# Merged gate halves: turned by TensorE, or moved in 32 wide blocks by three DMA queues and turned by VectorE

## The chip, the core and the metric

The kernel runs on one core of one Trainium2 chip. TensorE, VectorE (DVE), ScalarE (ACT), GpSimd (POOL) and SyncE (SP) each run their own list of instructions in order and meet at semaphores. The metric is the device time of one execution in microseconds (us); lower is better.

## What is computed

Two layers of a decoder trunk, 256 tokens of width 1024, all in float32. The change lies in the middle of each layer, where two branches are gated, added and projected:

```python
z = h @ w_in[l]
y_a = gmlp_branch(...) @ gm_w_proj[l]
y_b = mla_branch(...) @ mla_w_proj[l]
gates = jax.nn.sigmoid(z[..., OFF_GATE:].reshape(B, S, N_BRANCHES, D))
merged = gates[..., 0, :] * y_a + gates[..., 1, :] * y_b
x = x + merged @ w_out[l]
h2 = rms_norm(x, ffn_norm_g[l])
if l % 2 == 0:
    x = x + swiglu(h2, ...)            # dense, layer 0
else:
    x = x + moe_swiglu(h2, ...)        # top 2 of 8 experts, layer 1
```

## The kernel before

**Products.** Each float32 matrix is held as a high part (rounded to the matmul's type) and a low part (the rest), and a product is three passes: high x high, low x high, high x low. Weights come in chunks of 128 x 2048 numbers. SyncE loads a chunk into a ring of raw slots, ScalarE copies it to `w_hi` (`split_hi`, line 549), VectorE subtracts to get `w_lo` (`split_lo`, line 554), and TensorE multiplies (`one_pass`, line 619). In the mixer a chunk holds four 128-row tiles for a strip of 512 columns, so it is 2 (token tiles) x 4 x 3 = 24 matmuls. `w_hi` and `w_lo` have three slots: the copy of chunk n + 3 waits until TensorE is done with chunk n (`chunk_used`). A raw slot is loaded again when the subtraction of its last chunk is done (`lo_done`).

**Order.** `plan` is one hand-written list of steps. TensorE, ScalarE and VectorE each walk it in order and do their share of every step. `mul(l, what, j, k0, then, inside)` adds a chunk to the plan: the matmuls, then the steps of `then`, then `("split", ...)` for the chunk three further on. GpSimd and SyncE have programs of their own.

**The stretch in question.** Tokens lie on the partitions, 128 x 2 tiles. The last projection `pb` gives two strips (halves) of 512 columns. `evac("pb", j)` on VectorE (lines 2004 to 2013) scales strip j by its gate and adds it to `vbuf`, and raises `merged_b`. The product with `w_out` needs the operand with its 1024 columns on the partitions, so each half must be turned. `("merged_turns", l, half)` does that: TensorE turns eight 128 x 128 tiles into two PSUM banks (line 1018, through `turn4`, line 932), ScalarE copies them with the factor 0.5 to `act_hi` (line 1419), VectorE subtracts to `act_lo` (line 1866). Half 0 is turned after chunk `pb(1, 0)`, half 1 after chunk `wo(0, 0)`. The four chunks of `w_out` are multiplied in the order (strip 0, rows 0 to 511), (strip 1, rows 0 to 511), (strip 0, rows 512 to 1023), (strip 1, rows 512 to 1023); the first two read half 0 of the operand, the last two half 1.

**Who else hangs on it.** In layer 0, GpSimd waits for `merged_b`, clears `ws_raw` and stores it 18 times to `x_rows` and `y_rows` in HBM (lines 868 to 880), before it moves the hidden blocks of the dense layer for VectorE to turn (line 888). In layer 1 it waits for `merged_b` and loads the router's weights `wr`, `br` (lines 892 to 896), for which the step `("router", l)` of ScalarE and VectorE waits. SyncE's first expert load into memory that the mixer used waits until half 1 of layer 1 has been turned (lines 531, 532).

Of the kernel before, what the change touches and what calls it, by code (L numbers as in the profile page):

```python
# [34 lines left out]
P = 128  # L35
# [23 lines left out]
def decoder_trunk(nc, x, mix_norm_g, w_in, gm_v_norm_g, gm_v_norm_b, gm_w_spatial, gm_b_spatial, gm_w_proj,  # L59
# [72 lines left out]
    keys_in = {}  # L132

    def mul(l, what, j, k0=0, then=(), split=True, inside=()):
# [15 lines left out]
        else:  # L150
# [19 lines left out]
    for l in range(L):  # L170
# [113 lines left out]
    with ExitStack() as ctx:  # L284
# [53 lines left out]
        def part(n):  # L338
# [43 lines left out]
        vv = sb("vv", [P, TT, H, DV], F32, mixer)  # L382
        ws_t = sb("ws_t", [P, NG, P], F32, mixer)
# [92 lines left out]
            sem("scores_done"), sem("max_ready"), sem("exp_done"), sem("prob_ready"))  # L476
        merged_b, sig_done = sem("merged_b"), sem("sig_done")
# [10 lines left out]
        chosen_ready, gap_ready, places_read, counts_ready = (  # L488
            sem("chosen_ready"), sem("gap_ready"), sem("places_read"), sem("counts_ready"))
# [7 lines left out]
        class Ring:  # L497
# [23 lines left out]
            def wait_slot(self, sp, e, j):  # L521
# [105 lines left out]

        def turns_in(step):
            return {"norm_turns": 2, "latent_turns": 2 - step[2] if step[0] == "latent_turns" else 0, "spatial_weights": 2, "mix_tokens": 2, "merged_turns": 2,
# [36 lines left out]
        def operand_turns(l, what, k0):  # L666
# [8 lines left out]
                    "wo": lambda: last_turn["merged_turns", l, half]}.get(what, lambda: None)()  # L675
# [50 lines left out]
        def _(sp):  # L726
# [19 lines left out]

            for n in range(2):
# [1523 lines left out]
```

## Time and profile before

| | |
|---|---|
| median of 3 runs | 1414.89 us (1413.83 to 1415.05) |
| the profiled execution | 1415.23 us |
| its span, first to last instruction | 1413.5 us |
| TensorE matmul / weight load busy | 99% / 82% |
| VectorE, ScalarE, GpSimd busy | 83%, 67%, 12% |
| granted TensorE clock, mean | 0.999 |
| bytes moved | 424.32 MB, 300 GB/s |

How to read it: the expert phase takes about the last 750 us of the span, the two mixers and the dense layer the rest. In the views PE is TensorE's matmuls, PEld its weight loads, SPq the queue of SyncE. A row of a timeline is start, duration, engine, line, operation, output<-inputs, count, and in brackets the idle time before it and what ended it. Where neighbours are merged, the duration is that of the group.

### The profile page before, as it was taken

The page shows a single profiled execution, that of the slowest core. Times are in us where ns is not written, and L with a number is a line of the kernel's source. Part 1 is how long each engine was busy: PE and PEld are TensorE (multiplying, and loading weights), DVE is VectorE, ACT ScalarE, POOL GpSimd, SP SyncE. Part 2 cuts the span into 40 slices and gives each one's busy share as a digit, 9 for nine tenths or more (in the row PEclk, how much of TensorE's full clock was granted, in tenths as well). Part 3 has the DMA queues.
Part 4 walks back from the last instruction along what each step waited for, and adds up shares of the span by engine and source line. Part 5 has one row for each costly group of instructions (what it writes and reads, how often), then busy time and mean ns, then how long its engine had stood idle before and what let it go on. Part 6 is the DMA issues. An engine that isn't in the chain of part 4 may idle for free.

```text
span 1413.5 us, 19089 instructions
## 1 busy us (share of the span) xinstructions
PE 1404.5 (99%) x6567; PEld 1159.6 (82%) x6567; DVE 1167.7 (83%) x1197; ACT 950.0 (67%) x966; POOL 172.1 (12%) x305
## 2 busy tenths in 40 slices
PE   9999999999999999999999999999999999999998
PEld 7888778888888888788888888888888888888886
DVE  6998766676557899667989898898988988999986
ACT  6678645445435677644777777777777777778774
POOL 2032003476600050000300000000000000000010
PEclk9999999999999999999999999999999999999999
DMA  9476549976666484558999999999999999999995
GB/s 338 163 217 207 179 150 332 300 228 201 200 222 206 155 245 128 194 179 314 330 355 410 365 396 408 373 390 405 351 410 372 385 405 365 393 371 393 409 374 188
DMA packets 171636, 424.32 MB, mean 300 GB/s; under 512 B 19436, under 2 KB 50792, under 8 KB 171544
## 3 DMA queue, kind: packets, MB, share of 16 engines
q1 hardware_dynamic: 157128, 393.42, 76.7%
q0 software_dynamic: 13376, 26.16, 6.1%
q10 hardware_dynamic: 1040, 3.68, 0.6%
q8 instruction: 38, 0.62, 0.2%
q14 instruction: 54, 0.44, 0.1%
HBM read 398.20 MB, written 15.81 MB: 293 GB/s over the span
## 4 chain that ended last, share of the span: by engine, by line
PE 96%; DMA 2%; DVE 1%; ACT 0%; SPq 0%; issue 0%; DVEq 0%; ACTq 0%
PE ps L619 89%; DMA raw_more<-in_moe_w_down 1%; PE ps L1194 1%; PE ps L1053 1%; PE ps L1062 1%; PE ps L932 1%; PE ps L1051 1%; PE ps L1037 1%; PE ps L1010 0%; PE ps L976 0%; DMA raw<-in_w_in 0%; DVE w_lo L554 0%; ACT w_hi L549 0%; PE ps L1035 0%; PE ps L1186 0%; SPq L537 0%
## 5 line engine op out<-in xcount | busy, mean ns | idle before, releaser
L554 DVE TENSOR_TENSOR w_lo<-raw,w_hi 128x2048 fp32r<-128x2048 f32 (+3 forms) x184 | 383.7, 2092 | 78.0 <-ACT w_hi L549 76.9
L549 ACT ACTIVATE w_hi<-raw 128x2048 fp32r<-128x2048 f32 (+3 forms) x184 | 322.2, 1758 | 123.7 <-PE ps L619 97.5
L619 PE MATMUL ps<-w_hi,act_hi 128*128 128x512 f32 (+1 forms) x1264 | 332.4, 391 | 0.6 <-DVE w_hi L1803 0.5
L619 PE MATMUL ps<-w_hi,act_lo 128*128 128x512 f32 (+1 forms) x1264 | 328.5, 387 | 0.0
L619 PE MATMUL ps<-w_lo,act_hi 128*128 128x512 f32 (+1 forms) x1264 | 326.8, 387 | 0.0
L619 PEld LDWEIGHTS ps<-w_lo,act_hi 128*128 128x128 f32 x1264 | 235.8, 188 | 48.2
L619 PEld LDWEIGHTS ps<-w_hi,act_lo 128*128 128x128 f32 x1264 | 235.6, 188 | 48.0
L619 PEld LDWEIGHTS ps<-w_hi,act_hi 128*128 128x128 f32 x1264 | 233.1, 188 | 46.9 <-ACT act_hi L1337 1.2
L554 DVE TENSOR_TENSOR w_lo<-raw_more,w_hi 128x2048 fp32r<-128x2048 f32 (+1 forms) x96 | 201.8, 2110 | 30.4 <-ACT w_hi L549 30.4
L549 ACT ACTIVATE w_hi<-raw_more 128x2048 fp32r<-128x2048 f32 (+1 forms) x96 | 170.0, 1775 | 56.1 <-PE ps L619 46.8
L554 DVE TENSOR_TENSOR w_lo<-raw_low,w_hi 128x2048 fp32r<-128x2048 f32 (+1 forms) x64 | 137.6, 2156 | 13.4 <-ACT w_hi L549 12.7
L549 ACT ACTIVATE w_hi<-raw_low 128x2048 fp32r<-128x2048 f32 (+1 forms) x64 | 115.9, 1810 | 38.2 <-PE ps L619 33.4
L554 DVE TENSOR_TENSOR w_lo<-raw_lent,w_hi 128x2048 fp32r<-128x2048 f32 (+3 forms) x56 | 119.9, 2140 | 19.5 <-ACT w_hi L549 19.4
L549 ACT ACTIVATE w_hi<-raw_lent 128x2048 fp32r<-128x2048 f32 (+3 forms) x56 | 100.6, 1797 | 32.2 <-PE ps L619 31.6
L619 PE MATMUL ps<-w_hi,ehid_hi 128*128 128x512 f32 x352 | 96.6, 392 | 0.0
L619 PE MATMUL ps<-w_lo,ehid_hi 128*128 128x512 f32 x352 | 95.8, 390 | 0.4 <-DVE w_lo L554 0.4
L619 PE MATMUL ps<-w_hi,ehid_lo 128*128 128x512 f32 x352 | 95.8, 389 | 0.0
L888 POOL DMA_DIRECT2D hid_blocks<-hid x176 | 86.0, 497 | 62.5 <-DVE hid L2031 48.5
L913 POOL DMA_INDIRECT xres<-y_rows,row_i x4 | 8.2, 2050 | 670.4 <-PE ps L619 670.4
L619 PEld LDWEIGHTS ps<-w_lo,ehid_hi 128*128 128x128 f32 x352 | 65.9, 188 | 14.9 <-DVE w_lo L554 1.3
L619 PEld LDWEIGHTS ps<-w_hi,ehid_lo 128*128 128x128 f32 x352 | 66.1, 188 | 13.9
L619 PEld LDWEIGHTS ps<-w_hi,ehid_hi 128*128 128x128 f32 x352 | 65.4, 188 | 13.1
(296 smaller groups left out, 1353.3 us busy)
## 6 DMA issues: line engine op xcount, KB each, us to landing
raw<-in_moe_w_gu SPq DMA_DIRECT2D x96, 512.0 KB, 11.7
raw_more<-in_moe_w_down SPq DMA_DIRECT2D x80, 512.0 KB, 10.9
raw<-in_w_in SPq DMA_DIRECT2D x66, 512.0 KB, 5.4
raw_low<-in_moe_w_gu SPq DMA_DIRECT2D x64, 512.0 KB, 12.1
raw_more<-in_moe_w_gu SPq DMA_DIRECT2D x64, 512.0 KB, 12.3
raw<-in_moe_w_gu SPq DMA_DIRECT2D x48, 384.0 KB, 8.4
raw<-in_dense_w_gu SPq DMA_DIRECT2D x34, 512.0 KB, 5.3
raw_lent<-in_moe_w_gu SPq DMA_DIRECT2D x32, 512.0 KB, 11.3
```

The lines of the kernel that those rows point to most:

```text
L549: nc.scalar.activation(w_hi[:, self.split_slot(j), 0:n], self.raw(j)[:, 0:n], ACT.Copy).then_inc(self.hi, 1)
L554: nc.vector.tensor_tensor(w_lo[:, c, 0:n], self.raw(j)[:, 0:n], w_hi[:, c, 0:n].bitcast(F32), ALU.subtract).then_inc(self.lo, 1)
L619: return nc.tensor.matmul(dst, a, b, start=start and n == 0, stop=stop and n == 2)
L888: pool.dma_start(hid_blocks[32 * c:32 * c + 32, j % 2, b, :], hid_by_block[32 * b:32 * b + 32, j % 2, c, :, :, :]).then_inc(hid_moved[j % ...
L913: pool.indirect_dma_start(xres[:, t, :], None, y_row_list, bass.IndirectOffsetOnAxis(ap=row_i[:, 1, c, t:t + 1], axis=0), compute_op=ALU.a ...
L932: mm = nc.tensor.transpose(bank[:, i * P:(i + 1) * P], src(i // TT, i % TT), ident)
L1037: nc.tensor.matmul(dst.rearrange("p (t q) -> p t q", t=TT), vv[:, t, 2 * n + hh, :], first_keys[hh], start=True, stop=False)
L1051: nc.tensor.matmul(ps[:, 6, hh * P:(hh + 1) * P].rearrange("p (b i) -> p b i", b=4), q_h[:, 0:P], k_h[:, 0:4, :], start=True, stop=True)
L1053: mm = nc.tensor.matmul(ps[:, 7, hh * S:(hh + 1) * S].rearrange("p (b i) -> p b i", b=8), q_h[:, P:S], k_h, start=True, stop=True)
L1062: mm = nc.tensor.transpose(bank[:, q * P:(q + 1) * P], probs[pair % 2][:, blk * P:(blk + 1) * P], ident)
L1194: mm = nc.tensor.transpose(turn_banks(j)[:, k * P:(k + 1) * P], ehid[:, k * P:(k + 1) * P], ident)
```

## The change

The halves are no longer turned by TensorE. VectorE writes the sum of the gated strips not to `vbuf` but to `merged_by_block`, a view of `u_buf` in which the columns are ordered by blocks of 32. Sixteen DMAs a half, each 32 partitions x 1 KB, move the blocks to their place in `merged_turned`, a view of `qb`: three of them issued by GpSimd, six by SyncE, seven by ScalarE. VectorE then turns every 32 x 32 block with one transpose of 128 x 1024 in place (`merged_blocks`); ScalarE copies the result to `act_hi` and VectorE subtracts to `act_lo` (`merged_split`). The factor 0.5 is applied when the product with `w_out` is added to `x`. GpSimd's fill in layer 0 waits for the second transpose, SyncE's first expert load into mixer memory for `m_lo`. Two semaphores of the router are made one.

The diff, without declarations, the router's semaphores and the removed branches of `merged_turns`:

```diff
+        if (what, k0) == ("wo", 4):
+            moves_at[l, j] = len(chunks) - 1
...
         mul(l, "pb", 0, 4, [evac("pb", 0)])
-        mul(l, "pb", 1, 0, [("merged_turns", l, 0)])
-        mul(l, "pb", 1, 4, [evac("pb", 1)])
-        mul(l, "wo", 0, 0, [("merged_turns", l, 1)] + [("router", l)] * (l % 2))
-        mul(l, "wo", 1)
+        plan.append(("merged_moves", l, 0))
+        mul(l, "pb", 1, 0, [("merged_blocks", l, 0)])
+        mul(l, "pb", 1, 4, [("merged_split", l, 0), evac("pb", 1)])
+        plan.append(("merged_moves", l, 1))
+        mul(l, "wo", 0, 0, [("router", l)] * (l % 2))
+        mul(l, "wo", 1, 0, [("merged_blocks", l, 1), ("merged_split", l, 1)])
...
-                    wait_turn_read(sp, last_turn["merged_turns", L - 1, 1])
-                    wait_turn_read(sp, last_turn["merged_turns", L - 1, 1] - 1)
+                    sp.wait_ge(m_lo, 2 * L)
...
+        def merged_move(j, n):
+            b, c = n // 4, n % 4
+            return merged_turned[32 * c:32 * c + 32, j, b, :, :, :], merged_by_block[32 * b:32 * b + 32, j, c, :, :, :]
...
+            def move_merged(l, j):
+                sp.wait_ge(merged_b, 2 * l + j + 1)
+                if j:
+                    sp.wait_ge(m_turned, 2 * l + 1)
+                for n in range(3, 9):
+                    sp.dma_start(*merged_move(j, n)).then_inc(m_moved, 16)
...
+            moves = {at + 2 + j: (l, j) for (l, j), at in moves_at.items() if l < L - 1}
             for n in range(RAW, N0):
+                if n in moves:
+                    move_merged(*moves[n])
                 static_load(n)
...
+                    if not q and is_first(e) and c in (0, 2):
+                        move_merged(L - 1, c // 2)
                     r.load(sp, e, c, [(to[:, 0:w], g), (to[:, w:2 * w], u)])
...
+                for j in range(2):
+                    pool.wait_ge(merged_b, 2 * l + j + 1)
+                    if j:
+                        pool.wait_ge(m_turned, 2 * l + 1)
+                    for n in range(3):
+                        pool.dma_start(*merged_move(j, n)).then_inc(m_moved_pool, 16)
                 if not l:
-                    pool.wait_ge(merged_b, 2)
+                    pool.wait_ge(m_turned, 2)
...
+                    merged = what == "wo" and not j
                     if not first:
+                        if merged:
+                            pe.wait_ge(m_hi, 2 * l + k0 // 4 + 1)
...
+                        elif p == 1 and not cell and merged:
+                            pe.wait_ge(m_lo, 2 * l + k0 // 4 + 1)
...
+                elif kind == "merged_moves":
+                    j = step[2]
+                    act.wait_ge(merged_b, 2 * l + j + 1)
+                    for n in range(9, 16):
+                        act.dma_start(*merged_move(j, n)).then_inc(m_moved, 16)
+                elif kind == "merged_split":
+                    j = step[2]
+                    act.wait_ge(m_turned, 2 * l + j + 1)
+                    for t in range(TT):
+                        op = copy(act_hi[:, 4 * j:4 * j + 4, t * P:(t + 1) * P].rearrange("p k (b i) -> p k b i", b=4),
+                                  merged_turned[:, j, :, t].rearrange("p b k i -> p k b i"))
+                    op.then_inc(m_hi, 1)
...
+                elif kind == "merged_blocks":
+                    j = step[2]
+                    dve.wait_ge(m_moved, 16 * 13 * (2 * l + j + 1))
+                    dve.wait_ge(m_moved_pool, 16 * 3 * (2 * l + j + 1))
+                    nc.vector.transpose(merged_moved[:, j], merged_moved[:, j]).then_inc(m_turned, 1)
+                elif kind == "merged_split":
+                    j = step[2]
+                    dve.wait_ge(m_hi, 2 * l + j + 1)
+                    for t in range(TT):
+                        k, cols = slice(4 * j, 4 * j + 4), slice(t * P, (t + 1) * P)
+                        op = tt(act_lo[:, k, cols].rearrange("p k (b i) -> p k b i", b=4),
+                                merged_turned[:, j, :, t].rearrange("p b k i -> p k b i"),
+                                act_hi[:, k, cols].bitcast(F32).rearrange("p k (b i) -> p k b i", b=4), ALU.subtract)
+                    op.then_inc(m_lo, 1)
...
-                            tt(vbuf[:, :, cols], vbuf[:, :, cols], gate_b[j], ALU.add).then_inc(merged_b, 1)
+                            for t in range(TT):
+                                op = tt(merged_by_block[:, j, :, t].rearrange("p c k i -> p k c i"),
+                                        *(v.rearrange("p (k c i) -> p k c i", k=4, c=4)
+                                          for v in (vbuf[:, t, cols], gate_b[j][:, t, :])), ALU.add)
+                            op.then_inc(merged_b, 1)
...
-                            tt(xres[:, t, cols], xres[:, t, cols], bank[:, t, :], ALU.add).then_inc(free if t else x_added, 1)
+                            stt(xres[:, t, cols], bank[:, t, :], 0.5, xres[:, t, cols], ALU.mult, ALU.add
+                                ).then_inc(free if t else x_added, 1)
```

## Rows read from the trace of the kernel before

**Rows 1.** The page, part 1: busy time and share of the span.

```profile
PE 1404.5 (99%) x6567; PEld 1159.6 (82%) x6567; DVE 1167.7 (83%) x1197; ACT 950.0 (67%) x966; POOL 172.1 (12%) x305
```

**Rows 2.** Waits of TensorE, longest first: total us, times, longest us.

```profile
PE ps L949 <- POOL consts L823: 1.8, 1, 1.8
```

**Rows 3.** The chain that ended last, in order of time: start us, us, what.

```profile
212.16 10.92 PE ps L619 x48
223.07 0.87 PE ps L932 x8
...
665.82 32.67 PE ps L619 x144
```

**Rows 4.** Timeline of layer 0, from the merge of half 0 to w_out.

```profile
207.21 1.22 DVE L2013 TENSOR_TENSOR vbuf<-vbuf,ws_raw 128x1024 f32<-128x1024 f32 x1
...
211.76 1.09 ACT L1337 ACTIVATE act_hi<-ps 128x512 fp32r<-128x512 f32 x2 [3.90 <-PE ps L932]
...
212.39 1.29 DVE L1712 SCALAR_TENSOR_TENSOR act_lo<-ps,act_hi 128x512 fp32r<-128x512 f32 x2 [1.76 <-ACT act_hi L1337]
...
217.47 1.98 PE L619 MATMUL ps<-w_hi,act_hi 128*128 128x512 f32 x8
```

**Rows 5.** Timeline of layer 0, around the merge and turn of half 1.

```profile
217.74 1.22 DVE L2010 SCALAR_TENSOR_TENSOR ws_t<-ws_t,ps 128x1024 f32<-128x1024 f32 x1 [0.76 <-PE ps L619]
...
220.28 0.96 POOL L872 MEMSET ws_raw<- 128x1024 f32 x1 [107.19 <-DVE vbuf L2013]
...
224.52 1.92 ACT L549 ACTIVATE w_hi<-raw 128x2048 fp32r<-128x2048 f32 x1
...
226.47 2.29 DVE L554 TENSOR_TENSOR w_lo<-raw,w_hi 128x2048 fp32r<-128x2048 f32 x1 [1.01 <-ACT w_hi L549]
```

**Rows 6.** Timeline of layer 1, from the merge of half 1 on.

```profile
633.30 1.23 DVE L2013 TENSOR_TENSOR vbuf<-vbuf,ws_t 128x1024 f32<-128x1024 f32 x1
...
634.82 0.92 POOL L894 DMA_DIRECT2D wr<-in_moe_w_router x1 [107.56 <-DVE vbuf L2013]
...
635.73 0.56 POOL L895 DMA_DIRECT2D br<-in_moe_b_router x1
...
638.83 0.42 ACT L1337 ACTIVATE counting<-consts 128x256 fp32r<-128x256 f32 x1
...
644.68 2.19 SPq L537 DMA_DIRECT2D raw_low<-in_moe_w_gu  x4
```

**Rows 7.** Lines 770 and 1671: DMA issues, ns min/median/max, first and last start.

```profile
L770 SPq DMA_DIRECT2D xs<-x_rows x28: 317/332/1483, 717.0 to 1266.1; - x28
...
L1671 ACTq DMA_DIRECT2D y_rows<-y_sb x7: 343/350/388, 761.2 to 1314.8; - x7
```

**Rows 8.** Line 888, 330 to 345 us: GpSimd's moves of 16 KB.

```profile
L888 POOL DMA_DIRECT2D hid_blocks<-hid x22: 496/496/498, 329.9 to 342.9; - x22
...
DMA to landing us min/median/max: 1.6/2.4/4.1
```

**Rows 9.** Line 1828: VectorE's transpose of 128x1024, ns.

```profile
L1828 DVE STREAM_TRANSPOSE ws_t<-ws_raw x1: 1237/1237/1237, 393.1 to 393.1; 128x1024 f32<-128x1024 f32 x1
```

**Rows 10.** Line 895: the load of `br`, issue to landing.

```profile
DMA to landing us min/median/max: 2.9/2.9/2.9
```

**Rows 11.** Timeline of GpSimd's last fill store, its landing (line 879), first hidden block.

```profile
231.44 0.55 POOL L879 DMA_DIRECT2D y_rows<-ws_raw  x1
...
DMA to landing us min/median/max: 24.2/24.2/24.2
...
274.93 0.71 DVE L1873 STREAM_TRANSPOSE hid_blocks<-hid_blocks 128x512 f32<-128x512 f32 x1 [1.30 <-DMA hid_blocks<-hid]
```

**Rows 12.** Stretches at the end: PE busy first, then PEclk, DMA share, GB/s last.

```profile
1408.00:1409.00 1.00, 0.14 (x1) 0.00 (x0) 0.75 (x2) 0.00 (x0) 0.00 (x0) 1.00 0.74 256
...
1411.00:1412.00 1.00, 0.00 (x0) 0.00 (x0) 0.00 (x0) 0.00 (x0) 0.00 (x0) 0.66 0.52 186
```

More of the change, by code:

```diff
@@ L132, in decoder_trunk @@
     keys_in = {}
+    moves_at = {}
     def mul(l, what, j, k0=0, then=(), split=True, inside=()):
@@ L476, in decoder_trunk @@
             sem("scores_done"), sem("max_ready"), sem("exp_done"), sem("prob_ready"))
+        m_moved_pool, m_moved, m_turned, m_hi, m_lo = sem("m_moved_pool"), sem("m_moved"), sem("m_turned"), sem("m_hi"), sem("m_lo")
         merged_b, sig_done = sem("merged_b"), sem("sig_done")
@@ L487, in decoder_trunk @@
         hid_turned, hid_copied, hid_split = sem("hid_turned"), sem("hid_copied"), sem("hid_split")
[L488 to L489 removed]
+        routed_by_dve, places_read, counts_ready = sem("routed_by_dve"), sem("places_read"), sem("counts_ready")
+        CHOSEN_READY, GAP_READY = 1, 2
         pass_sems = []
@@ L625, in three @@
             return nc.tensor.matmul(dst, a_hi, b_lo, start=False, stop=stop)
+        def merged_move(j, n):
+            b, c = n // 4, n % 4
+            return merged_turned[32 * c:32 * c + 32, j, b, :, :, :], merged_by_block[32 * b:32 * b + 32, j, c, :, :, :]
         def turns_in(step):
-            return {"norm_turns": 2, "latent_turns": 2 - step[2] if step[0] == "latent_turns" else 0, "spatial_weights": 2, "mix_tokens": 2, "merged_turns": 2,
+            return {"norm_turns": 2, "latent_turns": 2 - step[2] if step[0] == "latent_turns" else 0, "spatial_weights": 2, "mix_tokens": 2,
                     "a_turns": 2, "values": 1, "prob_turns": 2}.get(step[0], 0)
@@ L674, in operand_turns @@
                     "pb": lambda: last_turn["values", l, 4 * half + 3],
-                    "wo": lambda: last_turn["merged_turns", l, half]}.get(what, lambda: None)()
+                    }.get(what, lambda: None)()
         def turned_q(head):
@@ L1017, in _ @@
                         turn4(b0 + b, lambda k, t: vbuf[:, t, (4 * j + 2 * b + k) * P:(4 * j + 2 * b + k + 1) * P])
-                elif kind == "merged_turns":
-                    half = step[2]
-                    pe.wait_ge(merged_b, 2 * l + half + 1)
-                    for b in range(2):
-                        c = 4 * half + 2 * b
-                        turn4(b0 + b, lambda k, t: vbuf[:, t, (c + k) * P:(c + k + 1) * P])
                 elif kind == "values":
@@ L1418, in _ @@
                         turn_hi_parts(b0 + b, t1_hi, 4 * step[2] + 2 * b, 1.0)
-                elif kind == "merged_turns":
-                    for b in range(2):
-                        turn_hi_parts(b0 + b, act_hi, 4 * step[2] + 2 * b, 0.5)
+                elif kind == "merged_moves":
[10 more added lines that the diff above has]
+                    op.then_inc(m_hi, 1)
                 elif kind == "hidden_turn":
@@ L1865, in _ @@
                         turn_lo_parts(bb, t1_hi, t1_lo, 4 * step[2] + 2 * b, 1.0)
-                elif kind == "merged_turns":
-                    for b in range(2):
-                        turn_lo_parts(b0 + b, act_hi, act_lo, 4 * step[2] + 2 * b, 0.5)
+                elif kind == "merged_blocks":
[12 more added lines that the diff above has]
+                    op.then_inc(m_lo, 1)
                 elif kind == "hidden_blocks":
@@ L2069, in _ @@
                     top_i[:, :, 0:2].rearrange("p t (j o) -> p j t o", o=1).to_broadcast([P, 2, TT, E]), ALU.is_equal))
-            tt(chosen[:], one[:, 0], one[:, 1], ALU.add).then_inc(chosen_ready, 1)
-            dve.wait_ge(chosen_ready, 1)
-            tt(rt[:, :, 0], top[:, :, 1], top[:, :, 0], ALU.subtract).then_inc(gap_ready, 1)
+            tt(chosen[:], one[:, 0], one[:, 1], ALU.add).then_inc(routed_by_dve, 1)
+            dve.wait_ge(routed_by_dve, CHOSEN_READY)
+            tt(rt[:, :, 0], top[:, :, 1], top[:, :, 0], ALU.subtract).then_inc(routed_by_dve, 1)
             link(tt(picked_scale[:], chosen[:, :, 0].bitcast(F32), small[:, 2:4], ALU.mult))
```

7 lines of the change are left out of this document (5 added, 2 removed).

## The prediction, written before the changed kernel ran

> **What bounds the kernel now.** I read the page's busy times first: TensorE 99% [rows 1]. The waits of TensorE confirm it: the longest is 1.8 us at the very start, and nothing else it waits for reaches 1 us [rows 2]. So an edit pays only by what it takes off TensorE, and costs only where it makes TensorE wait. Then the chain of work in order of time, for TensorE's pace: 48 matmuls in 10.92 us, or 5.46 us for a chunk of 24 [rows 3]. Last the timelines of the two stretches from the first merged half to the router [rows 4 to 6], for what stands in VectorE's and ScalarE's queues while TensorE works. I write M1 and M2 for the moments at which half 0 and half 1 are merged (`merged_b`), P for the first matmul of the first w_out chunk, A-2 to A+1 for the chunks wo(0,0), wo(1,0), wo(0,4), wo(1,4), and A-4, A-3 for the two pb(1) chunks ahead of them.
>
> **What goes.** Four groups of eight turns, one for each half and layer. A group is 0.87 us [rows 3], and each stands between two busy chunks. 4 x 0.87 = 3.48 us is all that the change can win. The copies out of PSUM on ScalarE and VectorE go too, but copies of the same size from SBUF replace them: nothing either way. The w_out evacuation with a factor 0.5 is one instruction for one: nothing, bounded by the cover (TensorE has later chunks to work on).
>
> **Half 0.** M1 was 207.21 + 1.22 = 208.43, P was 217.47 [rows 4]. One group of turns between them goes, so P = M1 + 8.17.
> - Issues: SyncE's 128 KB moves take 0.32 us each, ScalarE's store 0.35 [rows 7], GpSimd's moves 0.50 [rows 8], after a start some 0.29 us late (633.30 + 1.23 against 634.82, [rows 6]). So 6 x 0.32 = 1.9, 7 x 0.35 = 2.45, 3 x 0.50 + 0.29 = 1.8 us side by side; ScalarE's seventh starts about M1 + 2.2.
> - Landing: the trace has no SBUF to SBUF move of 32 KB by SyncE or ScalarE. Nearest is the 16 KB move of GpSimd, 1.6/2.4/4.1 us from issue to landing in a stretch with nothing else in flight but loads [rows 8]. I take 2.4, so all is landed at M1 + 4.6. Bounds: 1.6 us (M1 + 3.8), and, if SyncE's and ScalarE's 13 issues shut each other out (the last starts at M1 + 4.0) and a landing takes 3.1, between the median and the longest, M1 + 7.1.
> - VectorE's transpose of 128x1024 takes 1.24 us [rows 9], to M1 + 5.9; ScalarE's two copies of 128x512 about 1.15 (1.09 for two from PSUM, [rows 4]), to M1 + 7.05. TensorE wants them at M1 + 8.17: hidden, 1.1 us to spare.
> - VectorE then splits chunk A-1 (2.29 us, [rows 5]), which stood in its queue behind the transpose, to M1 + 8.2, and only then writes the low parts (1.3 us for two, [rows 4]) to M1 + 9.5. TensorE's second pass wants them at P + 1.8 = M1 + 10.0: hidden, with 0.5 us to spare.
> - But those low parts stand ahead of the pb(1) evacuation on VectorE, which could have begun at P + 0.27 [rows 5]. It begins at P + 1.3, and takes 1.22 us [rows 5] and 1.3 for the addition in two pieces (as the low parts). M2 = P + 3.9, where it was P + 2.75.
>
> The Trainium skill (DMA: Bandwidth & Descriptors, Anatomy of one DMA) gives about 2.0 us fixed and bytes/436e3 us for one DMA; by that 32 KB would land after 2.1 us and half 0 would be whole at M1 + 4.3, which leaves this part as it is. The same page (the table of choices at its end) speaks against the spread: DMAs issued by SyncE, ScalarE and GpSimd run on the same 16 engines, and spreading them saves issue time alone. The measured landings are 1.6 to 4.1 us, so they agree at their lower end.
>
> **Half 1, where it is decided.** TensorE has two chunks (A-2, A-1) between P and the chunk that reads half 1, so it wants the high parts at P + 10.9. In the plan, `merged_blocks` 1 and `merged_split` 1 stand behind chunk wo(1,0). VectorE's queue ahead of them holds the split of A+1, and that split needs ScalarE's copy, which needs TensorE to be done with A-2 (its slot of w_hi). Before, the copy ran at 224.52 and the subtraction at 226.47 [rows 5].
> - ScalarE now waits for M2 ahead of its seven issues: P + 3.9 to P + 6.4. Then the copy of A+1 (1.92 us, [rows 5]) to P + 8.4; without the issues P + 5.7 to 7.6.
> - VectorE subtracts A+1 to P + 10.7. The moves landed at M2 + 4.6 = P + 8.5, so it is the queue that is late, not the DMA.
> - Transpose to P + 12.0, two copies on ScalarE to P + 13.2. TensorE stalls 13.2 - 10.9 = **2.3 us**. The low parts (P + 14.5) are hidden by the first pass.
> - Lower bound, with landings at 1.6 us in half 0: M2 = P + 3.1, the issues no longer in the way, 1.5 us. Even with a free M2 the order of the queues alone gives 7.6 + 2.3 + 1.24 + 1.15 - 10.9 = 1.4. Upper bound, by M1 + 7.1: 6.4 us over the two halves.
>
> **Layer 1 has more in that queue.** GpSimd used to issue the router's weights right at M2 (634.82, its second load at 635.73, [rows 6]), landed 2.9 us after the second issue [rows 10]. Now its three moves go first: 0.29 + 1.5 + 0.92 + 2.9 = M2 + 5.6 = P + 9.5. Both ScalarE and VectorE wait for it in the step `router`, ahead of the split of A+1. ScalarE: 0.42 us of `counting` [rows 6], then the copy to P + 11.9; VectorE's subtraction to P + 14.2; transpose to 15.4; copies to 16.6. Stall **5.7 us**, lower bound (M2 = P + 3.1) 4.9, upper 8.2.
>
> **Other parts.** SyncE's moves stand ahead of the loads of A+2 and A+4 and, in layer 1, of expert chunks 0 and 2. Six of them take 1.9 us, and the loads behind them wait for splits that end later (that of A-2 after M1, that of A after M2): nothing; without that cover 1.9 us on a load that is read three chunks later, nothing too. The first load into memory shared with the mixer (644.68, [rows 6]) now waits for `m_lo`, at about P + 18 = 649. The expert phase begins near 665 [rows 3] and reads this slot as its fifth, four chunks of 12 matmuls or 11 us later: nothing. The fill of the expert rows starts when half 1 is turned, P + 12.0 instead of 220.28 [rows 5]: 8.7 us later. Its last store was issued at 231.44 and landed after 24.2 us, at 255.6 [rows 11]; now about 264.3, and the first moves of the hidden blocks queue behind it, 1.3 us later than they could start. VectorE waited for them before (1.3 us, [rows 11]) and will wait about 2.6. The copy of weights that waits behind that is for a chunk that TensorE reads only after two more (10.9 us). Nothing taken, up to 2 us in the range if loads come late beside the fill.
>
> **Sum.** -3.48 + 2.3 + 5.7 = +4.5 us. The profiled execution took 1415.23 us (span 1413.5 and 1.7 around it), 0.34 over the median of the three, 1414.89. Made against the profile 1419.7; as a median 1419.4.
>
> **The rivals.**
> - Slower still, one mechanism: landings. SyncE and ScalarE share what issues a DMA, so that 13 issues take 4.3 us, and half 0 itself is late (high parts at M1 + 9.6). Then -3.48 + 6.4 + 8.2 = +11.1, 1426. It decides from a landing at M1 + 5.1, where the low parts meet TensorE. For it: issues stretched to 1.48 us where queues are full [rows 7]. Against: the queues are near empty here. Chance 0.12.
> - The clock. At the end of the trace TensorE stops at 1408.14; its granted clock is 1.00 in 1408 to 1409 and 0.66 in 1411 to 1412 [rows 12], so a pause of some 3 us lets it fall from 2.4 to 1.2 GHz. A stall of 5.7 us would do that. How long it stays there no row shows; for half a chunk to one chunk at half rate the cost is 2.7 to 5.4 us at most, and 1.5 if it returns soon: 1421 to 1424. The Trainium skill (TensorE: Matmul & The Clock Gate, Part 1) states the same two levels and a return after sustained work. Chance 0.18.
> - About even: the router's loads aren't in the way (they land sooner, or the copy of A+1 does not suffer), and layer 1 stalls like layer 0. -3.48 + 2 x 2.3 = +1.1, down to -3.48 + 2 x 1.4 = -0.7: 1414.2 to 1416.0. For it: wr and br are small. Against: the times in [rows 6, 10], and a queue kept in order. Chance 0.24.
> - The other side: half 1 is ready in time and all of 3.48 us stays, 1411.4. It decides on the split of A+1: only if ScalarE and VectorE had it done by P + 8.4 would the transpose and the copies fit before P + 10.9. Before, that split ended 226.47 + 2.29 = 228.76, after the second group of turns; without them it can't end before P + 9.9. Chance 0.06.
>
> **How the numbers follow.** Forecast 0.40, own range 1417.5 to 1421. Slower by over 0.2% (2.8 us, about what a measurement can tell from no change) are the forecast, the landings and the clock: 0.70. Within: 0.24. Faster: 0.06. The range from 1415.3 to 1424.5 leaves out the faster case, the lower half of the even case and the upper end of the landings.
>
> **What would show it.** Right: TensorE idle before wo(0,4) in both layers, released by `act_hi`, about 2.3 and 5.7 us, none before wo(0,0); transpose 1 right behind the subtraction of A+1; in layer 1 ScalarE waiting for the router's loads before `counting`. Wrong: no idle time there (then order or durations of the queues are read wrongly); idle before wo(0,0) (landings); a granted clock under 1 behind the layer 1 stall; waits for weights between 250 and 280 (the fill).

## The result and the profile after

The change makes the kernel slower: 1433.73 us (1431.85 to 1435.68) against 1414.97 us (1413.83 to 1415.48) for the kernel before beside it, a ratio of 1.0136 with a 95% interval of 1.0123 to 1.0149, or +18.8 us. The forecast was +4.5, and its range ended at 1424.5. The profiled execution took 1431.85 us, span 1430.1; the one of before took 1415.23, span 1413.5, so the two traces differ by 16.6 us; the rows below say where they come from.

The page of the changed kernel: the busy times, and of the costliest groups (busy, mean ns; idle before and its releaser) the three that answer best to the change. TensorE's share is still 99%, since four waits in 1430 us hardly move it.

```profile
PE 1409.8 (99%) x6535; PEld 1162.8 (81%) x6535; DVE 1172.0 (82%) x1205; ACT 949.8 (66%) x966; POOL 177.9 (12%) x317
...
L627 PE MATMUL ps<-w_hi,act_hi 128*128 128x512 f32 (+1 forms) x1264 | 339.0, 397 | 12.4 <-ACT act_hi L1367 12.3
L627 PE MATMUL ps<-w_hi,act_lo 128*128 128x512 f32 (+1 forms) x1264 | 329.7, 388 | 0.0
...
L919 POOL DMA_DIRECT2D hid_blocks<-hid x176 | 86.0, 497 | 56.7 <-DMA y_rows<-ws_raw 22.1
```

What TensorE waited for in the changed kernel (us in total, times, longest). Against [rows 2] one row is new, and everything else follows from it: four waits for the high parts, one ahead of each chunk that opens a half, in each layer.

```profile
PE ps L627 <- ACT act_hi L1367: 12.3, 4, 4.4
PE ps L980 <- POOL consts L848: 1.8, 1, 1.8
```

The timeline of layer 0 in the changed kernel (start, duration, engine, line, operation; in brackets the idle time before it and its end), answering to [rows 4, 5]. M1 is 208.97, where the second addition of L2063 ends; the moves begin at 209.00.

```profile
209.00 3.99 SPq L765 DMA_DIRECT2D qb<-u_buf  x6
209.00 4.96 ACTq L1453 DMA_DIRECT2D qb<-u_buf  x7
209.26 1.02 POOL L898 DMA_DIRECT2D qb<-u_buf  x2 [95.68 <-DVE u_buf L2063]
...
213.04 8.89 SPq L545 DMA_DIRECT2D raw<-in_dense_w_gu  x4
...
214.07 1.92 ACT L557 ACTIVATE w_hi<-raw 128x2048 fp32r<-128x2048 f32 x1 [5.74 <-issue]
...
217.57 1.25 DVE L1908 STREAM_TRANSPOSE qb<-qb 128x1024 f32<-128x1024 f32 x1 [6.39 <-DMA qb<-u_buf]
...
220.04 3.78 PE L627 MATMUL ps<-w_hi,act_hi 128*128 128x512 f32 x8 [2.85 <-ACT act_hi L1367]
...
223.35 1.29 DVE L2063 TENSOR_TENSOR u_buf<-vbuf,ws_t 128x512 f32<-128x512 f32 x2
...
229.94 1.92 ACT L557 ACTIVATE w_hi<-raw 128x2048 fp32r<-128x2048 f32 x1 [8.14 <-issue]
...
231.88 2.29 DVE L562 TENSOR_TENSOR w_lo<-raw,w_hi 128x2048 fp32r<-128x2048 f32 x1 [5.04 <-ACT w_hi L557]
...
234.10 1.24 DVE L1908 STREAM_TRANSPOSE qb<-qb 128x1024 f32<-128x1024 f32 x1
...
236.57 3.55 PE L627 MATMUL ps<-w_hi,act_hi 128*128 128x512 f32 x8 [2.52 <-ACT act_hi L1367]
...
243.58 1.07 PE L627 MATMUL ps<-w_hi,act_hi 128*128 128x512 f32 x4
```

Three things are to be seen. Half 0 is whole only at M1 + 8.6 (217.57), and TensorE waits 2.85 us for it. Half 1 stands behind the split of A+1, as forecast: the transpose at 234.10 follows the subtraction of 231.88 with no idle time. And ScalarE loses 5 us to its seven issues each time (209.00 + 4.96); the second time they hold up the copy of A+1 until 229.94.

Layer 1 in the same timeline: the first row is the wait for half 0, the others are half 1, with M2 at 646.99. This answers to [rows 6, 10].

```profile
642.39 3.68 PE L627 MATMUL ps<-w_hi,act_hi 128*128 128x512 f32 x8 [2.50 <-ACT act_hi L1367]
...
647.02 4.66 ACTq L1453 DMA_DIRECT2D qb<-u_buf  x7
...
649.66 0.56 POOL L926 DMA_DIRECT2D br<-in_moe_b_router  x1
...
652.63 0.42 ACT L1367 ACTIVATE counting<-consts 128x256 fp32r<-128x256 f32 x1 [8.49 <-DMA br<-in_moe_b_router]
...
657.10 1.24 DVE L1908 STREAM_TRANSPOSE qb<-qb 128x1024 f32<-128x1024 f32 x1
...
659.57 3.67 PE L627 MATMUL ps<-w_hi,act_hi 128*128 128x512 f32 x8 [4.43 <-ACT act_hi L1367]
```

Of ScalarE's 8.49 us without an instruction 4.66 are its seven issues; they end at 651.68, and the wait for `br`, issued at 649.66, is the last 0.95 us.

The issues of half 0 in layer 0, one row for each line (duration in ns, minimum, median, maximum); the landing times are ScalarE's. They answer to [rows 7, 8], which had 317/332 ns for SyncE and 343/350 for ScalarE.

```profile
L765 SPq DMA_DIRECT2D qb<-u_buf x6: 588/594/779, 209.0 to 212.4; - x6
...
L1453 ACTq DMA_DIRECT2D qb<-u_buf x7: 617/639/860, 209.0 to 213.3; - x7
...
DMA to landing us min/median/max: 1.9/2.2/4.2
```

And the granted clock in the first wait and behind it, then inside the first matmuls behind each of the other three (stretch; its length, busy us of PE, PEld, DVE, ACT, POOL; then the clock, DMA share, GB/s), where [rows 12] had shown 0.66 only at the end of the program.

```profile
217.00:220.00 3.00, 0.19 (x1) 0.00 (x0) 2.43 (x2) 1.16 (x3) 0.00 (x0) 0.87 0.33 118
220.00:223.00 3.00, 2.96 (x7) 2.38 (x8) 3.00 (x4) 1.79 (x1) 0.00 (x0) 0.50 0.26 57
223.00:226.00 3.00, 3.00 (x8) 2.32 (x8) 2.97 (x4) 0.00 (x0) 1.06 (x3) 0.50 0.91 306
...
238.00:239.00 1.00, 1.00 (x4) 0.79 (x3) 0.65 (x1) 0.31 (x1) 1.00 (x3) 0.50 1.13 422
643.00:644.00 1.00, 1.00 (x4) 0.81 (x3) 1.00 (x3) 1.00 (x1) 0.00 (x0) 0.50 0.00 0
...
660.00:661.00 1.00, 1.00 (x3) 0.73 (x3) 0.84 (x2) 1.00 (x1) 0.00 (x0) 0.50 1.05 426
```

The clock went to its lower level, 1.2 GHz, at each of the four waits. The four chunks behind them took 8.41, 7.01, 7.15 and 7.14 us where 5.46 is the full pace: 7.9 us together. The four waits cost, reckoned to the start of the matmuls, 2.99, 2.66, 2.64 and 4.57 = 12.9 us. With the turns gone: 12.9 + 7.9 - 3.5 = 17.3. To this comes a start of this stretch 0.5 us later in this execution (M1 is 208.97 and was 208.43), which makes 17.8. The first matmul of the last w_out chunk of layer 1, before and after, agrees:

```profile
648.99 1.07 PE L619 MATMUL ps<-w_hi,act_hi 128*128 128x512 f32 x4
```

```profile
666.71 1.07 PE L627 MATMUL ps<-w_hi,act_hi 128*128 128x512 f32 x4
```

They are 17.7 us apart, and the spans 16.6: 1.1 us comes back behind this point, by a cause not followed further. So the rows account for the loss up to there. They do not yet say what each cause is worth, since a cause that is taken away may only let the next one show; the experiments do.

### The profile page after: what moved, and what is told of

The parts are those of the page before. It is cut to its first block, busy times and chain, and to the rows that moved or that the text cites. A ratio compares the mean times of both kernels' runs of the same rounds, so it can differ in the third digit from the quotient of the medians.

```text
span 1430.1 us, 19092 instructions
## 1 busy us (share of the span) xinstructions
PE 1409.8 (99%) x6535; PEld 1162.8 (81%) x6535; DVE 1172.0 (82%) x1205; ACT 949.8 (66%) x966; POOL 177.9 (12%) x317
## 4 chain that ended last, share of the span: by engine, by line
PE 95%; DVE 2%; ACTq 1%; DMA 1%; issue 1%; ACT 1%; POOL 0%; DVEq 0%; POOLq 0%
PE ps L627 87%; PE ps L1224 1%; PE ps L1078 1%; ACTq L1453 1%; PE ps L1087 1%; PE ps L1076 1%; PE ps L1062 1%; DMA qb<-u_buf 1%; PE ps L1007 1%; PE ps L1041 0%; PE ps L963 0%; DVE u_buf L2063 0%; DVE qb L1908 0%; PE ps L980 0%; ACT w_hi L557 0%
## 5 line engine op out<-in xcount | busy, mean ns | idle before, releaser
L627 PE MATMUL ps<-w_hi,act_hi 128*128 128x512 f32 (+1 forms) x1264 | 339.0, 397 | 12.4 <-ACT act_hi L1367 12.3
L627 PEld LDWEIGHTS ps<-w_hi,act_hi 128*128 128x128 f32 x1264 | 237.1, 191 | 61.3 <-ACT act_hi L1367 14.5
L562 DVE TENSOR_TENSOR w_lo<-raw_low,w_hi 128x2048 fp32r<-128x2048 f32 (+1 forms) x64 | 137.5, 2155 | 11.7 <-ACT w_hi L557 10.9
```

The lines of the kernel that those rows point to most:

```text
L562: nc.vector.tensor_tensor(w_lo[:, c, 0:n], self.raw(j)[:, 0:n], w_hi[:, c, 0:n].bitcast(F32), ALU.subtract).then_inc(self.lo, 1)
L627: return nc.tensor.matmul(dst, a, b, start=start and n == 0, stop=stop and n == 2)
```

## The experiments

Each is measured beside its own runs of the kernel before; "+" is the median over theirs.

### The clock: keep TensorE busy in the waits

```diff
                         if merged:
+                            keep_busy(38 if (l, k0) == (L - 1, 4) else 22, 4)
                             pe.wait_ge(m_hi, 2 * l + k0 // 4 + 1)
```

> The changed kernel, with TensorE turning the identity into a free PSUM bank before each of its four waits for act_hi (22 turns, 2.4 us, at three of them, 38 turns, 4.1 us, at the last), so that it is not idle there. Theory (the waits cost twice: 12.3 us of idle time, and 7.9 us in which the matmuls behind them ran at half the granted clock): the operand comes at the same moments, the clock stays at 1.00, and the time falls by 7 to 8.5 us, to about 1425. Rival (the matmuls behind the waits were slow for another reason, such as weights or low parts that came late): no change, 1433.

1431.64 us, +17.1, ratio 1.0117 (1.0100 to 1.0134). The timeline of this kernel (the last row is VectorE's transpose of half 1 in layer 1), and then its clock in layer 0:

```profile
217.06 2.56 PE L980 MATMUL ps<-consts 128*128 128x128 f32 x22
219.96 2.11 PE L627 MATMUL ps<-w_hi,act_hi 128*128 128x512 f32 x8 [0.33 <-ACT act_hi L1368]
...
235.97 2.11 PE L627 MATMUL ps<-w_hi,act_hi 128*128 128x512 f32 x8 [2.01 <-ACT act_hi L1368]
...
241.54 1.07 PE L627 MATMUL ps<-w_hi,act_hi 128*128 128x512 f32 x4
...
657.22 1.25 DVE L1909 STREAM_TRANSPOSE qb<-qb 128x1024 f32<-128x1024 f32 x1 [1.96 <-DMA qb<-u_buf]
```

```profile
220.00:223.00 3.00, 2.92 (x12) 2.09 (x13) 3.00 (x4) 1.71 (x1) 0.00 (x0) 1.00 0.29 74
```

The clock stayed at full speed through the first three waits, and the chunk wo(0,0) took 5.99 us instead of 8.41. But wo(0,4) began at 235.97, only 0.6 us sooner than 236.57: the second half's chain runs from M2 on VectorE, ScalarE and the DMAs, and does not care how fast TensorE gets to the place where it waits. The full pace of wo(0,4) itself was won whole, so that wo(1,4) began at 241.54 instead of 243.58. In layer 0 the two slow chunks are thus 4.5 us in the rows and 2.0 us in the time.

Layer 1 can't be counted in the same way. wo(0,0) ended 3.3 us sooner than in the changed kernel (646.25 against 649.54), but the last move of half 1 landed 7.1 us after its issue, 12.3 us after M2 instead of 9.9; TensorE waited 3.7 us, the clock fell, and the chunk took 8.11 us. That profile is of the second slowest of four executions (1432.87 and 1433.36 against 1430.40 and 1430.41), so "+17.1" is a mixture, and the theory's 1425 was missed. What the clock costs in all is therefore not isolated; only layer 0's 2.0 us is.

### ScalarE issues nothing

SyncE takes moves 3 to 15, GpSimd 0 to 2.

```diff
-                for n in range(3, 9):
+                for n in range(3, 16):
                     sp.dma_start(*merged_move(j, n)).then_inc(m_moved, 16)
```

> ScalarE issues no moves, SyncE issues 13 of 16, GpSimd 3 as before. Theory (SyncE and ScalarE share what issues DMAs, so that an issue took 0.6 to 0.7 us with both and takes 0.32 with one): the 13 issues take about 4.3 us, the last lands about 6.5 us after the merge instead of 8.6, ScalarE's copies of weights start on time; TensorE's waits shrink to under 1 us for half 0 and about 2 to 4 for half 1; 1418 to 1422. Rival (a move of this shape costs 0.6 us to issue, whoever else issues): 13 issues take 7.8 us, the last lands 10 us after the merge, TensorE waits some 4 us before wo(0,0); 1433 to 1438.

1435.77 us, +21.2, ratio 1.0152 (1.0135 to 1.0168). The issues of SyncE alone:

```profile
L765 SPq DMA_DIRECT2D qb<-u_buf x13: 590/591/634, 208.5 to 216.2; - x13
...
DMA to landing us min/median/max: 1.8/1.8/2.6
```

With nobody beside it SyncE needs 0.59 us for one issue, as in the changed kernel. So the theory of shared issue falls and its rival holds; this is what an SBUF to SBUF move of 32 partitions costs here, and thirteen of them in a row end later (waits 16.3 us) than six beside seven. None of these landed late; in half 1 of layer 1, beside the router's loads, the longest took 3.4 us.

### Order: half 1 turned ahead of the split of A+1 and of the router

```diff
-        mul(l, "wo", 0, 0, [("router", l)] * (l % 2))
-        mul(l, "wo", 1, 0, [("merged_blocks", l, 1), ("merged_split", l, 1)])
+        mul(l, "wo", 0, 0, [("merged_blocks", l, 1), ("merged_split", l, 1)])
+        mul(l, "wo", 1, 0, [("router", l)] * (l % 2))
```

> merged_blocks and merged_split of half 1 are put behind chunk wo(0,0), ahead of the split of wo(1,4), and the router's step behind wo(1,0). Theory (half 1 waits for its place in VectorE's queue, behind the split of wo(1,4), and in layer 1 behind the router's loads): half 1 is turned as soon as its moves have landed, some 2 us earlier in layer 0 and 4 us in layer 1; with one or two of the falls of the clock gone, 1424 to 1428. Rival (the moves themselves are late for half 1 as they are for half 0): the wait in layer 0 stays above 2 us, and the gain is under 3 us, 1431 to 1433.

1432.79 us, +18.2, ratio 1.0136 (1.0114 to 1.0157): no better than the changed kernel, as the rival has it. In its timeline the transposes of half 1 are released by the moves:

```profile
232.49 1.25 DVE L1908 STREAM_TRANSPOSE qb<-qb 128x1024 f32<-128x1024 f32 x1 [6.40 <-DMA qb<-u_buf]
...
272.53 2.11 PE L627 MATMUL ps<-w_hi,act_hi 128*128 128x512 f32 x8 [2.82 <-DVE hid L2085]
```

M2 was 223.89 here, so the transpose stands at M2 + 8.6, where behind the split it stood at M2 + 9.5 (234.10 - 224.64). In layer 1 it began at 657.19, or M2 + 10.0, where it stood at M2 + 10.1 behind the router's step and the split. The queue that I had called the place of decision was worth 0.9 us in one layer and 0.1 in the other; the moves were nearly as late. And a wait came up that no kernel had before: 2.8 us for the first hidden strip of the dense layer.

### Ten moves by SyncE, six by GpSimd, with that order

> The order of the run before this one, with the moves issued by SyncE (10) and GpSimd (6) and none by ScalarE. Theory (shared issue): SyncE's ten take 3.2 us, GpSimd's six 3.3, all landed 5.5 us after the merge; half 0 is in time, half 1 late by 0.5 us at most, the clock stays up, and most of the 3.5 us of turns is won: 1411.5 to 1414. Rival (0.6 us a move in any case): landed after 8.2 us, waits of 2.5 us before wo(0,0) in both layers with falls of the clock, 1422 to 1428.

1430.74 us, +16.2, ratio 1.0111 (1.0094 to 1.0128). Half 0 was whole at M1 + 7.7; waits for the high parts 12.0 us, the hidden strip 2.8. Both the theory (under 1414) and its rival (1422 to 1428) were too low. Another division of sixteen issues brings a microsecond a half at most, not four.

### Moves that read HBM instead of SBUF

The source of each move is a block of `x` of the same shape, so the merged values are not used; all else runs as before.

```diff
-            return merged_turned[32 * c:32 * c + 32, j, b, :, :, :], merged_by_block[32 * b:32 * b + 32, j, c, :, :, :]
+            return (merged_turned[32 * c:32 * c + 32, j, b, :, :, :],
+                    x[0, 32 * b:32 * b + 32, 256 * c:256 * c + 256].rearrange("p (t k i) -> p t k i", t=TT, k=4))
```

> The changed kernel with the 64 moves reading 32 rows x 1 KB of the input x in HBM instead of the merged block in SBUF (the output is wrong for it; waits, destinations and order are the same). The runs before gave 0.59 us for an issue by SyncE alone, against 0.32 for SyncE's loads of gathered rows from HBM. Theory (it is the move from SBUF to SBUF that is slow to issue): 0.32 to 0.35 us an issue, all landed some 5 us after the merge, no wait before wo(0,0), the queue's wait of 2 to 3 us before wo(0,4) and 4 to 6 in layer 1; 1418 to 1423. Rival (a DMA of 32 rows of 1 KB takes 0.6 us to issue from anywhere): waits and time as in the changed kernel, 1431 to 1435.

1430.58 us, +17.0, ratio 1.0115 (1.0098 to 1.0132). ScalarE's issues and their landings:

```profile
L1454 ACTq DMA_DIRECT2D qb<-in_x x7: 365/452/832, 208.5 to 211.8; - x7
...
DMA to landing us min/median/max: 1.8/2.3/4.9
```

The issues were nearly a third cheaper (SyncE's median 0.42 us), and half 0 was hardly sooner: the transpose began at 216.67, M1 + 8.2, because ScalarE's last move, issued at 211.8, needed 4.9 us. In layer 1 `br` landed 5.6 us after its issue instead of 2.9, beside the moves, and TensorE waited 8.2 us. So a cheaper issue alone does not bring the half in: in the changed kernel ScalarE's seventh move was issued 2.2 us later than forecast and landed 1.8 us slower, about one half of the lateness each, and here the second part grew. The theory held on the issue in part, and not on the time.

### The fill started at M2, with the new order

> The order of e3 (half 1 turned ahead of the split of wo(1,4), router's step later), and the fill of the expert rows waits for merged_b as in the kernel before, right behind GpSimd's moves, not for the second transpose. Theory (in e3 the fill that starts some 12 us later took the loads of the dense weights past their time: one took 23.9 us, and TensorE waited 2.8 us for a hidden strip near 273): that wait goes, half 1 of layer 0 lands 1 to 3 us later beside the fill, 1427 to 1432. Rival (the wait near 273 is not the fill's): it stays.

1435.39 us, +21.9, ratio 1.0150 (1.0133 to 1.0167). The wait for the hidden strip was gone, as the theory has it, but the time lies above its 1427 to 1432. In layer 0 the last move of half 1 landed 7.5 us after its issue, its transpose began 10.7 us after VectorE was free, and TensorE waited 8.4 us. The fill of some 9 MB must not run beside the moves; its wait for the second transpose protects them.

### One half moved, the other turned by TensorE

In the first only half 0 is moved, in the second only half 1. The other half keeps its `merged_turns` as in the kernel before. Where half 1 is turned by TensorE, the fill starts at its merge again.

> Half 0 is moved and turned by VectorE, half 1 is turned by TensorE as before. If the cost of the change is the sum of its halves: waits of 2.5 to 3 us before wo(0,0) in both layers, each with a fall of the clock worth 1.7 us, less 1.7 us of turns: +6 to +9 us, 1421 to 1424. If the late evacuation behind half 0 is what makes half 1 late as well, the two single halves add up to clearly less than the changed kernel's +18.8.

> Half 1 is moved and turned by VectorE, half 0 is turned by TensorE as before. Sum of halves: waits of 3 to 3.5 us before wo(0,4) in layer 0 and 5 in layer 1, with falls of the clock, less 1.7 us of turns: +8 to +12 us, 1423 to 1427. Rival (half 1 is late only because half 0 delays it): waits under 1.5 us, 1415 to 1418.

Half 0 moved: 1419.53 us, +6.0, ratio 1.0046 (1.0029 to 1.0063), waits for the high parts 2.8 and 2.5 us among 5.9. Half 1 moved: 1424.42 us, +10.9, ratio 1.0075 (1.0058 to 1.0091), waits 3.4 and 4.7. Together 16.9 of the 18.8 us, which is the same within the intervals. So the halves cost nearly independently, and half 1 is late by itself, not because half 0 pushes M2 back.

### Twelve moves instead of sixteen

Four of the sixteen blocks (b = c) stay in their partitions. ScalarE copies these and issues nothing; SyncE and GpSimd move six each.

```diff
-            b, c = n // 4, n % 4
+            b = n // 3
+            c = n % 3 + (n % 3 >= b)
...
+                    for b in range(4):
+                        at = slice(32 * b, 32 * b + 32)
+                        op = copy(merged_moved[at, j, 256 * b:256 * b + 256],
+                                  merged_by_block[at, j, b].rearrange("p t k i -> p (t k i)"))
+                    op.then_inc(m_moved, 1)
```

> Only the 12 blocks that change partitions are moved, six by SyncE and six by GpSimd; the four on the diagonal (b equal to c) are copied by ScalarE, which issues no DMA. Everything else, the order of the plan too, is as in the changed kernel. Theory (the moves' own issue time, 0.59 us on SyncE and 0.50 on GpSimd, and ScalarE's last landings made half 0 late): all landed at merged + 5.5 us instead of + 8.6, the wait ahead of wo(0,0) falls from 2.5-2.85 us to 0 to 0.4, half 1 still waits behind the split of A+1: 1.5 us in layer 0 and, with six moves ahead of the router's weights, 5 to 6.6 us in layer 1. Sum about -3.5 + 0.4 + 1.5 + 6 + 1 of clock = +5.5 against the kernel before. Rival (landings beside weight loads are late whoever issues): landing still 4 us or more for the last move, waits ahead of wo(0,0) stay over 1.5 us, +12 or more.

1424.34 us, +9.2, ratio 1.0067 (1.0050 to 1.0084), where the changed kernel stood at +18.8. Its timeline:

```profile
208.45 3.84 SPq L766 DMA_DIRECT2D qb<-u_buf  x6
208.46 1.70 ACT L1368 ACTIVATE qb<-u_buf 32x256 f32<-32x256 f32 x4 [0.68 <-DVE u_buf L2071]
...
213.60 1.25 DVE L1916 STREAM_TRANSPOSE qb<-qb 128x1024 f32<-128x1024 f32 x1 [2.98 <-DMA qb<-u_buf]
```

```profile
639.04 0.56 POOL L927 DMA_DIRECT2D br<-in_moe_b_router  x1
...
651.20 3.78 PE L627 MATMUL ps<-w_hi,act_hi 128*128 128x512 f32 x8 [9.31 <-ACT act_hi L1368]
```

Half 0 whole at M1 + 5.2, and no wait for it in either layer. What is left is half 1 behind the plan: 1.42 us in layer 0 and 9.31 in layer 1, where `br` was issued behind six moves, landed 5.2 us later, and held up the split of A+1. The clock fell there, and the chunk took 8.31 us (651.20 to 659.51) instead of 5.46. By the rows 1.4 + 9.3 + 2.9 - 3.5 = 10.1, against the measured 9.2; as in the changed kernel, some of it comes back by the end.

### Twelve moves and the new order

Once with six and six moves, once with five by GpSimd, four by SyncE and three by ScalarE.

> The same 12 moves and four copies, and half 1 turned ahead of the split of A+1 and of the router. Theory: half 1 lands at merged + 5.5 us too, waits of TensorE for the high parts 0 to 0.6 us each, none over 1; if the 2.8 us wait for the hidden blocks at 272 us, seen with this order before, is there again, +1 us against the kernel before, else -2 us. Rival (the order gives nothing once the moves are quick, or the router's wait moves on to TensorE): no better than the kernel with the diagonal alone.

> As the kernel with 12 moves and the new order, but five moves by GpSimd, four by SyncE and three by ScalarE. If a move's landing depends only on the move (1.8 to 2.2 us), all is landed at merged + 5 us, half a microsecond sooner than with two queues. If what makes ScalarE's last moves late is that SyncE's 512 KB weight loads are issued before them (SyncE is done with its moves at + 2.4 us here, GpSimd issues until + 2.8), then the landings of the last moves of GpSimd or ScalarE stretch to 4 us and more, and this kernel is 1 to 4 us slower than the one with two queues.

1417.76 us, +2.6, ratio 1.0018 (1.0009 to 1.0028), and 1417.25 us, +2.1, ratio 1.0018 (1.0008 to 1.0027). The order that was worth nothing with late moves is worth 6.6 us with quick ones. Waits for the high parts are 1.6 us in the first and 0.65 in the second, where ScalarE's three moves are issued ahead of SyncE's next weight load and land in 2.1 to 2.9 us. The 2.8 us wait for the hidden strip is there in both, with a slow spell behind it. For the second kernel: -3.5 + 0.65 + 2.8 + 1.6 = +1.6.

### Where the wait for the hidden strip comes from

The next three kernels start from the one with twelve moves over three queues. First, the fill also waits for the split of A+1:

```diff
                     pool.wait_ge(m_turned, 2)
+                    pool.wait_ge(lo_done, moves_at[0, 1] + 1)
```

> Twelve moves over three queues with the new order, and GpSimd starts the fill of the expert rows only when the split of chunk A+1 of layer 0 is done as well, the moment at which SyncE issues the weight load that landed 18 to 24 us late beside the fill. Theory (that load stands behind the fill because the new order moved the split behind the transpose): the load lands in some 4 us, the 2.8 us wait for the hidden strip near 263 us and the clock loss behind it are gone, -4 against the same kernel without this wait, some -2 against the kernel before. Rival (any fill of 24 us at this place starves some load, or keeps the hidden blocks waiting): the wait only moves to a later chunk, no better than + 2.

1418.11 us, +3.3, ratio 1.0024 (1.0013 to 1.0035). The two loads behind the split landed in 4.0 and 5.1 us, as the theory has it (12.6 and 18.1 in the kernel without this wait), and the wait of 2.8 us that had ended at 265.81 was gone. But there were new ones:

```profile
275.03 2.11 PE L627 MATMUL ps<-w_hi,act_hi 128*128 128x512 f32 x8 [1.32 <-DVE hid L2094]
289.92 3.45 PE L627 MATMUL ps<-w_hi,act_hi 128*128 128x512 f32 x8 [3.71 <-DVE hid L2094]
```

The hidden blocks wait for the last store of the fill (idle 25.3 us before the first move), and a later fill delays them. The rival held: the wait only moved.

Second, the new order in layer 1 alone:

> Twelve moves over three queues, the new order in layer 1 alone; in layer 0 the split of A+1 stands ahead of the second transpose as in the changed kernel. Theory: no wait for the hidden strip at 263 us (the weight load goes out at 226.7 us, ahead of the fill), 1 to 1.5 us ahead of wo(0,4) in layer 0, none in layer 1: some -2 against the kernel before. Rival (the wait at 263 us comes from the later fill and not from the order of the load): 2.8 us there again, + 2 to + 3.

1417.56 us, +2.8, ratio 1.0019 (1.0010 to 1.0029). No wait for the hidden strip at all, but 3.56 us ahead of wo(0,4) in layer 0 instead of 1.42 in the kernel with ScalarE free: its three issues and four copies stand ahead of the copy of A+1, which begins at 224.92. The theory was right on the strip and wrong on the sum. Two loads go out here at 229.19 and 229.60, ahead of the fill's first store at 231.62, and land in 3.8 and 4.8 us; with the new order in layer 0 the next ones go out from 232.37 on, beside the fill that began at 228.33, and take 12.6 to 23.9 us. In both kernels the fill begins 0.07 us after wo(0,4) (231.55 and 228.26), so it is the place of the loads that differs. So the fill can cost in two ways, by the load that lies behind it (here and above) and by its own last store (the kernel before this one). That is read from the timelines and not isolated further.

What can be tested is the fill itself. Third and fourth, it goes out in pieces, two stores behind each strip's moves, on the kernel with twelve moves over three queues and the new order, and as a control on the kernel before:

```diff
+                        if j < E:
+                            for half in range(2):
+                                pool.dma_start(x_rows[j, half, :, 0:D], zeros).then_inc(rows_zeroed, 16)
...
```

> Twelve moves over three queues with the new order, and the fill in pieces: two of its stores behind each strip's moves of hidden blocks, instead of all 18 ahead of the first. Theory: no wait for the hidden strip and none for weights; only the 0.65 us ahead of wo(0,4) in layer 0 are left: -3.5 + 0.7 = -2.8 against the kernel before. Rival (hidden blocks queue behind 512 KB stores of their own queue): new waits of VectorE and TensorE for hid_blocks between 270 and 390 us, + 2 or more.

> The kernel before with its fill in pieces: two of its stores behind each strip's moves of hidden blocks. It tells how much of a gain of the kernel above is the fill's alone. Theory: TensorE waited for nothing at the fill in the kernel before, so no change within 0.2%. Rival: the fill costs something that the waits don't show (a matmul pace, a clock), and this one is faster by 1 us or more.

1411.67 us (1411.10 to 1412.21), -3.1, ratio 0.9978 (0.9968 to 0.9987): faster than both kernels. The control took 1414.62 us, ratio 0.9999 (0.9990 to 1.0009), no change. TensorE's waits in the faster kernel:

```profile
PE ps L982 <- POOL consts L849: 1.8, 1, 1.8
PE ps L627 <- ACT act_hi L1369: 0.7, 1, 0.7
```

-3.48 for the turns and +0.66 for one wait are -2.8, and -3.1 was measured. Nearly all of the 3.48 us that the change can win is to be had, given twelve moves, half 1 ahead of the split and the router, and a fill that is not one block of 9 MB.

## Why the prediction was wrong

**Right.** The direction; that 3.48 us of turns is all that can be won (the fastest kernel has 3.1 of them); that transpose 1 stands right behind the subtraction of A+1 (no idle before 234.10); that in layer 1 ScalarE waits for `br` ahead of `counting` (which ran at M2 + 5.6, as forecast).

**Right by luck: half 1.** Its waits were forecast at 2.3 and 5.7 us and measured at 2.5 and 4.4. But in layer 0 the transpose began at P + 17.1 and not P + 10.7 (P is 217.05 here, where TensorE would have begun wo(0,0)), and TensorE, held up and slowed in wo(0,0), wanted the half at P + 16.9 and not P + 10.9. Both moved by some 6 us, so the difference stayed. And the cause given, the order of the queues, was not needed: with the order changed the moves held the transpose to within 0.9 and 0.1 us of the same place.

**The issue time, mis-sized.** I took 0.32 and 0.35 us from [rows 7], which are loads from and stores to HBM. The moves took 0.59 and 0.64. That put ScalarE's seventh issue at M1 + 4.4 instead of M1 + 2.2. The value of GpSimd, 0.50 from [rows 8], was of the right kind and held (0.51). My reason for the upper bound, SyncE and ScalarE shutting each other out, was not borne out: SyncE alone needed 0.59.

**The last landing, mis-sized.** I took the median of [rows 8], 2.4 us, for all sixteen; the median was right (2.2) but the transpose waits for the last. For half 0 that took 4.2 and 4.0 us in the two layers, for half 1 3.9 and 5.8. The Trainium skill (DMA: Bandwidth & Descriptors, Anatomy of one DMA) gives about 2.0 us fixed for a DMA issued by GpSimd; GpSimd's three moves of half 0 in layer 0, at 1.8 to 2.3 us, agree. In the traces each move that took over 4 us was still on its way when SyncE's next 512 KB load began, or beside the fill. ScalarE's seventh is issued after that load in every half of the changed kernel. With twelve moves, all issued ahead of it, none took over 3.2. Where it is held is not shown, and no run isolates it. Both terms together, 2.2 us of issue and 1.8 of landing: all landed at M1 + 8.6 instead of M1 + 4.6, beyond my upper bound of M1 + 7.1. This is the step that failed: half 0 was not "hidden, 1.1 us to spare" but late by 2.99 us in layer 0 and 2.64 in layer 1. The rival of late landings, at 0.12, came nearest in what happened, though with the wrong cause, and its 1426 is still 8 us short.

**M2 and ScalarE.** ScalarE's issues blocked it for 5 us a half and not 2.45; M2 came at P + 7.6 and not P + 3.9, with half 0. The halves were yet nearly independent (+6.0 and +10.9): a late half 0 holds back M2 and TensorE alike.

**The clock.** I counted it as a rival for the 5.7 us stall alone; it fell at waits of 2.5 us too. The rows show 7.9 us of slow chunks. In layer 0, where keeping TensorE busy held the clock up in both waits, 4.5 us of them gave back 2.0; for layer 1 no run tells. This term was put at nothing in the forecast, and it is smaller than the rows alone would say.

**The fill.** "Nothing taken" was right for the changed kernel and right by luck: with the new order the same fill cost 2.8 us of waiting and 1.6 of clock. The rule of the Trainium skill weighed in the prediction (DMA: Bandwidth & Descriptors, Rules for kernel authors), that a spread over queues saves issue time alone, was no argument against the spread: issue time was part of what bound (thirteen moves on one queue: +21.2).

**In sum, by the rows.** Waits ahead of wo(0,0) 2.99 + 2.64 = 5.6 us, forecast 0; ahead of wo(0,4) 2.66 + 4.57 = 7.2, forecast 8.0; slow chunks 7.9, forecast 0. That is +12.7 on the forecast's +4.5, or some 17.3 in the traces; the medians are 18.8 apart.

## What to carry to other kernels

When many small DMAs gate one instruction, cost their issue from rows of the same kind of move (SBUF to SBUF, same partitions) and the landing by the longest in a stretch with the same neighbours, not by a median; and count an engine that issues as blocked meanwhile. Before moving blocks, ask which stay in place: four fewer of sixteen moves, with the order of the consumers' queues, took +18.8 to +2.1. Look also at what the shifted work collides with further on: a bulk store kept out of the way (in pieces) turned that into -3.1.

## What was not expected of the hardware

- An issue of a 32 KB SBUF to SBUF move takes SyncE 0.59 us and ScalarE 0.64, the same shape read from HBM 0.42 and 0.45, GpSimd 0.50 to 0.51.
- The granted clock fell to half at a wait of 2.50 us (layer 1, wo(0,0)). In the kernel with ten moves by SyncE and six by GpSimd it fell behind a wait of 1.94 us (0.50 in 220 to 221) and not behind one of 2.50 (1.00 in 233 to 236), and in the kernel with only half 1 moved TensorE went on at full pace (2.11 us for eight matmuls) after one of 3.37. The length of the pause alone does not decide it.
- A slow spell is cheap where TensorE soon waits again for something that other engines make, and costs in full where it does not: in layer 0 a chunk that was 2.4 us quicker brought 0.6 us, the next, 1.4 us quicker, brought 1.4.
